# Half stores and tile order at the end, constants behind the input, two splits moved, and the norms' bias on VectorE

## The reference

```python
# first block, per layer l
y = _mla(x, ...) if l == 0 else _swa(x, ...)
x = _layernorm(alpha * x + y, ln_mix_g[l], ln_mix_b[l])
x = _layernorm(alpha * x + _mlp(x, mlp_w_up[l], mlp_w_down[l]), ln_mlp_g[l], ln_mlp_b[l])
# second block
h = rmsnorm(x, g[0]);  proj = h @ w_in
y = (gm * (hm @ w_mlstm_out) + gd * (hd @ w_diff_out) + gr * (hr @ w_ret_out)) @ w_out
x = x + rmsnorm(y, g[1])
h2 = rmsnorm(x, g[2]);  a, u = split(h2 @ w_ffn_in)
x = x + rmsnorm((silu(a) * u) @ w_ffn_out, g[3])
```

## Time and profile before

| | |
|---|---|
| Median of 3 runs | 2545.45 us (2542.76 to 2547.97) |
| Profiled execution | 2543.65 us |
| its span in the trace | 2541.9 us |
| TensorE matmuls | 2452.6 us, 96% |
| TensorE weight loads | 2024.5 us, 80% |
| VectorE | 1114.9 us, 44% |
| ScalarE | 886.0 us, 35% |
| Pool | 114.6 us, 5% |
| DMA | 220.32 MB, mean 87 GB/s |

### The profile page before, as it was taken

The page is one execution under the profiler, slowest core; times in us unless marked ns, Lnnn a source line. Parts: engine busy times, 40 slices in busy tenths (PEclk is TensorE's granted clock), DMA queues, the critical chain, the costliest instruction groups (busy, mean ns, idle before and its releaser), DMA issues.

```text
span 2541.9 us, 29499 instructions
## 1 busy us (share of the span) xinstructions
PE 2452.6 (96%) x11784; PEld 2024.5 (80%) x11784; DVE 1114.9 (44%) x1487; ACT 886.0 (35%) x1444; POOL 114.6 (5%) x169
## 2 busy tenths in 40 slices
PE   7798999999989999998999999999999999999997
PEld 7577888888878788887888888888877788888886
DVE  3355633445665543346455322223245524433334
ACT  3232422323443332235444323332245534522222
POOL 3000200000100100000000000000000000000001
PEclk9999999999999999999999999999999999999999
DMA  5512332222311323322222222222321122322221
GB/s 161 75 54 67 117 100 100 90 92 83 108 42 50 118 98 100 99 100 67 78 71 81 92 92 83 83 83 84 104 67 50 51 94 80 108 99 91 96 94 67
DMA packets 187063, 220.32 MB, mean 87 GB/s; under 512 B 20531, under 2 KB 141568, under 8 KB 186832
## 3 DMA queue, kind: packets, MB, share of 16 engines
q1 hardware_dynamic: 183200, 206.13, 25.4%
q0 software_dynamic: 3760, 12.73, 2.4%
HBM read 213.60 MB, written 5.24 MB: 86 GB/s over the span
## 4 chain that ended last, share of the span: by engine, by line
PE 89%; DVE 6%; ACT 3%; issue 1%; DMA 1%; POOL 0%; SPq 0%; ACTq 0%; POOLq 0%; DVEq 0%
PE A L507 46%; PE B L507 40%; DVE WL L1754 2%; PE C L507 1%; ACT WH L1186 1%; DMA X<-in_x 1%; DVE Y L1912 1%; PE C L876 0%; PE C L1091 0%; DVE YL L1969 0%; DVE st L1893 0%; PE C L932 0%; ACT ar L1262 0%; DVE ar L1967 0%; ACT XH L1189 0%
## 5 line engine op out<-in xcount | busy, mean ns | idle before, releaser
L1754 DVE TENSOR_TENSOR WL<-RAW,WH 128x2048 fp32r<-128x2048 f32 (+1 forms) x197 | 448.8, 2278 | 690.1 <-ACT WH L1186 690.1
L1186 ACT ACTIVATE WH<-RAW 128x2048 fp32r<-128x2048 f32 (+1 forms) x197 | 370.9, 1883 | 626.0 <-PE A L507 561.1
L507 PE MATMUL B<-XH,WH 128*128 128x512 f32 (+1 forms) x1440 | 548.2, 385 | 8.7 <-DVE WL L1754 5.4
L507 PE MATMUL B<-XH,WL 128*128 128x512 f32 (+1 forms) x1440 | 539.9, 379 | 0.0
L507 PE MATMUL B<-XL,WH 128*128 128x512 f32 (+1 forms) x1440 | 526.5, 381 | 6.4 <-DVE XL L1769 6.3
L507 PE MATMUL A<-WH,YH 128*128 128x512 f32 x944 | 367.7, 390 | 1.6 <-DVE YL L2243 1.6
L507 PE MATMUL A<-WH,YL 128*128 128x512 f32 x944 | 367.3, 389 | 0.0
L507 PE MATMUL A<-WL,YH 128*128 128x512 f32 x944 | 367.2, 389 | 0.0
L507 PEld LDWEIGHTS B<-XH,WH 128*128 128x128 f32 x1440 | 271.8, 189 | 78.2 <-issue 16.4
L507 PEld LDWEIGHTS B<-XH,WL 128*128 128x128 f32 x1440 | 272.0, 189 | 51.3
L507 PEld LDWEIGHTS B<-XL,WH 128*128 128x128 f32 x1440 | 263.7, 190 | 57.1 <-DVE XL L1769 8.3
(11 more groups left out here) (290 smaller groups left out, 2125.9 us busy)
## 6 DMA issues: line engine op xcount, KB each, us to landing
RAW<-in_w_in SPq DMA_DIRECT2D x33, 1024.0 KB, 5.1
RAW<-in_mlp_w_up SPq DMA_DIRECT2D x32, 1024.0 KB, 5.2
RAW<-in_mlp_w_down SPq DMA_DIRECT2D x32, 1024.0 KB, 5.0
RAW<-in_w_in SPq DMA_DIRECT2D x48, 512.0 KB, 4.3
RAW<-in_w_ffn_in SPq DMA_DIRECT2D x22, 1024.0 KB, 5.1
RAW<-in_w_ffn_out SPq DMA_DIRECT2D x10, 1024.0 KB, 5.0
RAW<-in_mla_w_o SPq DMA_DIRECT2D x4, 1024.0 KB, 5.1
RAW<-in_swa_w_q SPq DMA_DIRECT2D x4, 1024.0 KB, 4.9
```

The source lines that it names most:

```text
L507: return nc.tensor.matmul(dst, l, r, start=first, stop=last)
L1186: nc.scalar.activation(WH[s][:, 0:n], RAW[s][:, 0:n], ACT.Copy).then_inc(hi_ready, 1)
L1754: tt(WL[s][:, 0:n], RAW[s][:, 0:n], f32(WH[s][:, 0:n]), ALU.subtract).then_inc(lo_ready, 1)
```

## The change

- Pool waits for x's last tile before it issues the constants, and loads GB only behind the roots of the latents.
- `plus_bias` moves to VectorE: one tile behind each up weight tile's pair of features in the first group of both MLPs; at the SWA border two tiles behind each of two splits. Pool only waits and reloads GB.
- At the border to the in-projection ("pre"), the split of the first mLSTM weight tile moves on VectorE between the two halves of XL's low parts, on ScalarE ahead of tile 3's square.
- At the border to the FFN ("post"), the four low parts of the first half of XL move ahead of tile 3's product.
- In the last down half TensorE takes the token tiles in the order (t, kh) = (0,0), (1,0), (0,1), (1,1), (2,0), (2,1), (3,0), (3,1). The root is made by ScalarE and VectorE in place of Pool. VectorE multiplies the first half of Y by its gain in h = 0 (`first_half`), behind ScalarE's squares, and its split of the last weight tile moves behind the fourth add of h = 0. `add_normed` works in halves, and each half is stored by itself.

```diff
@@ -494,9 +494,11 @@
-            sp.wait_ge(s_("fin_x"), t + 1)
-            sp.dma_start(out[0, tok(t), :], X[:, t, :]).then_inc(s_("stored"), 16)
-        sp.wait_ge(s_("stored"), 16 * T)
+            for h in range(2):
+                cols = slice(512 * h, 512 * h + 512)
+                sp.wait_ge(s_("fin_x"), 2 * t + h + 1)
+                sp.dma_start(out[0, tok(t), cols], X[:, t, cols]).then_inc(s_("stored"), 16)
+        sp.wait_ge(s_("stored"), 16 * 2 * T)
...
@@ -1160,12 +1162,27 @@
             c, use, done = c + tiles, use + tiles, done + tiles
-            for h in range(2):
+            for h in range(2 if n < 2 else 1):
                 for kh in range(2):
...
                     c += 1
+        pe.wait_ge(lo_ready, c + 1)
+        for t, kh in ((0, 0), (1, 0), (0, 1), (1, 1), (2, 0), (2, 1), (3, 0), (3, 1)):
+            nk = (4, 2)[kh]
+            wh, wl = grid(WH[slot(c + kh)], nk, 512), grid(WL[slot(c + kh)], nk, 512)
+            if kh == 0:
+                pe.wait_ge(a_free[t], ra + 5)
+            elif t == 0:
+                pe.wait_ge(lo_ready, c + 2)
+            for j in range(nk):
+                k = 4 * kh + j
+                r = mm3(A[t][:], YH[:, k, tok(t)], YL[:, k, tok(t)], wh[:, j, :], wl[:, j, :], k == 0, k == 5)
+            if t == 3:
+                r.then_inc(chunk_done, 1)
+            elif kh:
+                r.then_inc(tok_done, 1)
...
@@ -1429,11 +1446,11 @@
         over_root("pre", 2)
+        split(BASE["if"][0] + 1)
         then_root("pre", 3)
...
-        split(BASE["if"][0] + 1)
         act.wait_ge(s_("if_abs"), 1)
...
@@ -1732,6 +1749,10 @@
                                      scale=D ** -0.5, accum_out=stat(SS + 4 * h + t)).then_inc(s_("fin_ss"), 1)
+                if h:
+                    act.wait_ge(s_("fin_ss"), T + t + 1)
+                    act.wait_ge(s_("fin_half"), t + 1)
+                    nc.scalar.activation(stat(RS + t), stat(SS + 4 + t), ACT.Sqrt, bias=stat(SS + t)).then_inc(s_("fin_root"), 1)
...
@@ -1933,6 +1954,7 @@
                 lo_half("pre", 0, (2, 3), NG0, ALU.mult)
+                split(c + 1)
                 lo_half("pre", 1, range(4), NG0, ALU.mult)
...
@@ -1955,6 +1977,10 @@
+        def plus_bias(t, dst, signal):
+            tt(dst[:, t, :], Y[:, t, :], GB[:, 1, :], ALU.add).then_inc(signal, 1)
         def mlp(name, before, ln, n):
...
@@ -1967,6 +1993,8 @@
                         tt(YL[:, 2 * j + m, :], SQ_T[:, m, :], f32(YH[:, 2 * j + m, :]), ALU.subtract).then_inc(mlp_lo, 1)
+                    if first:
+                        plus_bias(j, Y, s_(before + "_y"))
                 for h in range(2):
...
@@ -1999,12 +2027,16 @@
         split(c0 + 1)
+        for t in range(2):
+            plus_bias(t, X, s_("ln1_x"))
         for m in range(2):
...
         split(c0 + 2)
+        for t in range(2, T):
+            plus_bias(t, X, s_("ln1_x"))
         dve.wait_ge(chunk_done, c0 + 2)
...
@@ -2059,7 +2091,6 @@
         c0, _, _, _, _, f0 = BASE["if"]
-        split(c0 + 1)
         nc.vector.memset(L_PRE, 0.0).then_inc(s_("ml_zero"), 1)
...
@@ -2304,6 +2335,8 @@
         for t in range(T):
+            if t == 3:
+                lo_half("post", 0, range(4), NG2, ALU.mult)
             product_out(1, t)
...
@@ -2315,18 +2348,24 @@
             elif t == 3:
-                lo_half("post", 0, (0, 1), NG2, ALU.mult)
                 root_inverse("post", 3)
-                lo_half("post", 0, (2, 3), NG2, ALU.mult)
                 lo_half("post", 1, range(4), NG2, ALU.mult)
-        def add_normed(name, gb, t, after):
-            if t == 0:
-                dve.wait_ge(gb_in, gb)
-            dve.wait_ge(s_(name + "_r"), t + 1)
-            then(stt(Y[:, t, :], Y[:, t, :], stat(RS + t), GB[:, 0, :], ALU.mult, ALU.mult))
-            tt(X[:, t, :], X[:, t, :], Y[:, t, :], ALU.add).then_inc(s_(after), 1)
+        def first_half(t):
+            dve.wait_ge(s_("fin_ss"), t + 1)
+            then(tt(Y[:, t, 0:512], Y[:, t, 0:512], GB[:, 0, 0:512], ALU.mult))
+            ts(stat(SS + t), stat(SS + t), RMS_EPS, None, ALU.add).then_inc(s_("fin_half"), 1)
+        def add_normed(t):
+            dve.wait_ge(a_free[t], ra + 6)
+            then(tt(xtmp[:, t % 2, :], Y[:, t, 512:1024], GB[:, 0, 512:1024], ALU.mult))
+            dve.wait_ge(s_("fin_root"), t + 1)
+            then(nc.vector.reciprocal(stat(RS + t), stat(RS + t)))
+            for h, y in enumerate((Y[:, t, 0:512], xtmp[:, t % 2, :])):
+                x = X[:, t, 512 * h:512 * h + 512]
+                stt(x, y, stat(RS + t), x, ALU.mult, ALU.add).then_inc(s_("fin_x"), 1)
...
@@ -2346,8 +2385,9 @@
             for h in range(2):
-                split(c + 1)
-                split(c + 2)
+                if n < 2 or h == 0:
+                    split(c + 1)
+                    split(c + 2)
                 for t in range(T):
...
@@ -2355,10 +2395,19 @@
                         tt(y, y, A[t][:], ALU.add).then_inc(a_free[t], 1)
-                    if n == 2 and h == 1 and t >= 1:
-                        add_normed("fin", 4 * 32 + 32, t - 1, "fin_x")
+                    if n == 2 and h == 0 and t == 0:
+                        dve.wait_ge(gb_in, 4 * 32 + 32)
+                    elif n == 2 and h == 0:
+                        if t == 3:
+                            split(c + 3)
+                        else:
+                            first_half(t - 1)
+                    elif n == 2:
+                        if t == 0:
+                            first_half(2)
+                            first_half(3)
+                        add_normed(t)
                 c += 2
-        add_normed("fin", 4 * 32 + 32, T - 1, "fin_x")
...
@@ -2378,6 +2427,8 @@
             return v.rearrange("(a n) -> a n", a=1)
+        pool.wait_ge(x_in[T - 1], 16)
...
@@ -2408,8 +2459,6 @@
-        load_gb(a["ln_mix_g"][0], a["ln_mix_b"][0])
         def over_root(dst, src, eps, signal):
...
@@ -2420,17 +2469,10 @@
+        load_gb(a["ln_mix_g"][0], a["ln_mix_b"][0])
         pool.wait_ge(consts_done, 1)
...
-        def plus_bias(ln, dst, signal):
-            pool.wait_ge(turned, turn(ln, KD))
-            for t in range(T):
-                tt(dst[:, t, :], Y[:, t, :], GB[:, 1, :], ALU.add).then_inc(signal, 1)
-        pool.wait_ge(chunk_done, BASE["mlp0"][0] + 1)
-        plus_bias("ln0", Y, s_("ln0_y"))
         pool.wait_ge(s_("ln0_y"), T)
...
@@ -2443,14 +2485,11 @@
         load_bias(1)
-        plus_bias("ln1", X, s_("ln1_x"))
         pool.wait_ge(s_("ln1_x"), T)
...
             load_bias(g)
-        pool.wait_ge(chunk_done, BASE["mlp1"][0] + 1)
-        plus_bias("ln2", Y, s_("ln2_y"))
         pool.wait_ge(s_("ln2_y"), T)
...
@@ -2479,16 +2518,8 @@
-        def root_of_halves(name, wait, t):
-            wait(t)
-            then(tt(stat(SS + t), stat(SS + t), stat(SS + 4 + t), ALU.add))
-            over_root(RS + t, SS + t, RMS_EPS, s_(name + "_r"))
         pool.wait_ge(s_("post_x"), T)
         load_gb(a["norm_gains_2"][0, 3])
-        for t in range(T):
-            root_of_halves("fin", lambda t: pool.wait_ge(s_("fin_ss"), T + t + 1), t)
...
```

## The result

| | median | range | runs |
|---|---|---|---|
| before | 2544.11 us | 2542.66 to 2547.97 | 4 |
| after | 2525.07 us | 2523.35 to 2526.57 | 4 |

The ratio is 0.9923, with a 95% interval of 0.9905 to 0.9940: 19 us less. The prediction was 2525.5 us.

What follows compares the result with a forecast made beforehand. TensorE, busy 2452.6 of 2541.9 us, was taken as the bound of nearly every stage. Terms 5.0 + 4.0 + 2.4 + 3.9 + 0.1 + 3.4 = 18.8 us gave 2524.9 from the profiled execution; forecast 2525.5, range 2518 to 2533.

Steps and rivals of the forecast that it cites:

- Start: Wait for x at the kernel's start: constants issued behind x let its tiles land earlier; 5.0 us, range 2 to 6.
- the rule: At the start: Pool's DMAs can starve beside two-port VectorE operations; constants would come late but within their cover, costing nothing.
- Bias: Both MLPs: bias adds on VectorE end TensorE's wait for a split stretched by Pool; 4.0 us in MLP 0, 2.4 in MLP 1.
- SWA border: Bias adds moved to VectorE at this border, where no TensorE wait stands: nothing gained, bounds -1 to +1 us.
- Border to the in-projection: Earlier split of the first mLSTM weight tile ends TensorE's wait for the gate op; 3.9 us, 2.2 if the clock falls anyway.
- FFN border: Low parts ahead of product 3: TensorE's wait is cut in two and moved; 0.1 us, bounds -0.5 to +0.5.
- The end: Tail behind the last matmul: VectorE's chain sets the end, with a new 2.6 us TensorE idle; 3.4 us gained.
- SP's slow queue (1): Rival at the start: SP's own queue is the slow one; 3 us less gain, 2528.5 us, chance 0.15.
- the missing wait (2): Rival at the end: the new wait is absent, tile 0 ends 2.6 us earlier; 2523 us, chance 0.12.
- the pushed split (3): Rival in both MLPs: VectorE's adds still push a split past TensorE's need; 6.4 us less, 2532 us, chance 0.08.
- the clock (4): Rival in the pair stage: TensorE's clock stays at the lower level for some 25 us; above 2550 us, chance 0.03.

Runs made afterwards that it cites:

- pool_dummy: The kernel after, with Pool also making four adds of the same size in MLP 0 that nobody needs; 2529.10 us.
- fix_post: The kernel after, with the low parts at the FFN border made in two pieces around the last product; 2527.75 us.
- u_pre: The kernel after, with the split at the in-projection border put back where before has it, on VectorE and ScalarE; 2528.11 us.
- fix_if: The kernel after, with ScalarE's split behind the gates' Exp and Ln and VectorE's behind the last gate operation; 2525.25 us.
- fix_end2: The kernel after, with VectorE's last weight split behind its second add and each tile finished behind the next tile's add; 2521.78 us.
- u_start: The kernel after, with the start of before: Pool issues the constants at once, ahead of x's tile 3; 2531.36 us.
- only_end: The kernel before, with nothing but the new end; 2538.03 us over ten runs.
- gb_only: The kernel before, with only the two GB loads moved behind Pool's roots; 2542.13 us.
- u_bias: The kernel after, with the three sets of four bias adds given back to Pool; 2534.66 us.

## Why the prediction held

The predicted 18.8 us stand against 19.6 us in the profiled pair and 19.0 in the medians. (The 2525.5 lies between 2524.9, from the profiled execution, and 2526.7, from the median; with a fourth run the median of before is 2544.11, 0.5 above the profiled one in place of 1.8.) Step by step:

**Start.** Predicted 5.0, with up to 1 us more; shown about 6, and 6.5 in the profiled pair (6.15 at the mark, where after has 1.7 us more of falls). The steps came 0.3 us late each: tile 3's transposes at 11.92 against 11.6, the first matmul at 13.84 against 13.5. What I had left in the range, that the first matmuls run at full rate at once, came true and is worth more than the 1 us: of the 6.5 us, 4.7 are the earlier first matmul and 1.9 the rate behind it. This term was mis-sized. The reasoning by bytes was right in direction and too neat: bytes at 285 GB/s give 3.0 of the 4.6 us, and GB, over half of the bytes, did nothing. In after the constants are issued from 11.6 to 22.2 us, at 0.49 to 0.70 us each beside VectorE's splits, no longer than in before (0.49 to 0.76). The prediction drew the rule too wide: the Trainium skill ("SBUF — State Buffer", Who interferes with whom) ties the starving to operations in a two-port mode and says that `tensor_tensor`, which these splits are, has none. The trace of after agrees. Nothing waited for a constant.

**Bias.** MLP 0 predicted 4.0, shown 4.4 with the SWA border, of which MLP 0 up to its last down product is 4.1; MLP 1 predicted 2.4, shown 2.5. The idle and the stretched split went as walked. The doubt in that step, whether the clock falls elsewhere instead, is answered below. The rows show what the stretch is: a stretched operation ends about its own length behind the Pool add beside it. In the earlier trace rows the last Pool add ends at 290.03 and the split, begun at 287.70, ends 2.15 us later (its own length is 2.29); in pool_dummy it is 283.42 and 1.08 us later (1.22). So what is added is the rest of a Pool add, here 2.2 us at most (2.88, 3.42 and 4.48 against 0.69, 1.22 and 2.29). The Trainium skill ("SBUF — State Buffer", SBUF: two separate sides) calls the sharing an exclusive lock held for the whole instruction, and the trace agrees.

**SWA border.** Predicted 0 (-1 to 1), and 0.3 shown. The -1.57 behind it is falls: that stretch takes 18.8 to 22.3 us in the fourteen profiled kernels, in no relation to their edits.

**Border to the in-projection.** Predicted 3.9, shown 1.8. This is the step that failed. I reckoned the gate operation a microsecond ahead of TensorE's need and stopped there; I did not ask what is late next. It is ScalarE's exponential, at the end of a chain from the gate operation over two weight splits and two scans. The chain moved by 1.8 us, and TensorE, 3.9 us earlier, waits 2.1 us for it. In the old order it waits 1.6 us there without a fall and not at all with one, so the fall's 1.7 us, a term of the 3.9, had cost nothing, and of the 2.2 us of idle 0.5 came back. That the profiled pair still showed 4.04 up to that point is chance: before had 5.1 us of falls there, 3.4 of them ahead of the idle, and after none.

**FFN border.** Predicted 0.1, shown 0.3, with the wait in two pieces as said (0.84 and 1.05).

**The end.** Predicted 3.4, between 4.0 without a fall behind the new idle and 2.8 with one; shown 3.7, without one. Sizes: the idle 2.33 us against 2.6, a tile 3.39 us against 3.25 (VectorE waits 0.46 us in each for ScalarE's root), the span's end 2.5 us behind the last write against 3.0. Counted from the last part's first matmul, the last write came 0.9 us later than reckoned, and the shorter time behind it gave 0.5 of that back. A fall behind the idle came in four other kernels: in fix_post, where it begins with the idle's end, it costs 1.2 us, as reckoned; in u_pre, pool_dummy and fix_if, where it begins 1.3 us later, 0.1 to 0.2 us. That VectorE's chain sets the end was right, and fix_end2 showed it to be VectorE's work even without its waits.

For the profiled pair the parts are 6.5 + 4.4 + 2.5 + 1.8 + 0.3 + 3.7 = 19.2 us, and the 0.4 us to its 19.6 are what falls come to elsewhere. That the sum came out is in part luck: the border's 2.1 us too much stand against 1.5 too little at the start, 0.4 in MLP 0, 0.1 in MLP 1, 0.2 at the FFN border and 0.3 at the end. Of the rivals, SP's slow queue (1) fell with u_start, the missing wait (2) with the 2.33 us, the pushed split (3) with the rows of MLP 0, and of the clock (4) nothing came beyond what moves any two runs apart.

## What to carry to other kernels

When an edit removes a wait, follow the work it releases to the same engine's next wait: a chain on two other engines can stand just behind, and a slow clock in the profiled run can hide it. Value an edit of a few microseconds by the stretch between two marks that both kernels have, at equal falls of the clock; here the whole time moves by 4 us for no reason of the edit. Compare the same matmul in both traces where no mark stands. Put an operation that waits for another engine behind the work that a third engine needs next, and keep Pool's long adds away from a VectorE whose work is due.

## What had not been expected of the hardware

**A fall that belongs to an idle.** The idle of 2.2 to 3.4 us in MLP 0 is followed by a fall of the granted clock in all five profiled kernels that have it (before, only_end, gb_only, u_bias, pool_dummy), and there is none there in the nine others. In windows of MLP 0 (busy time of PE, PEld, DVE, ACT and POOL with the instructions, then the granted clock, the DMA share and GB/s) u_bias has

```profile
286.00:291.00 5.00, 4.43 (x13) 3.50 (x14) 3.10 (x5) 2.97 (x4) 2.62 (x4) 0.68 0.96 298
```

and after

```profile
286.00:291.00 5.00, 5.00 (x24) 4.14 (x23) 4.69 (x4) 2.60 (x3) 0.00 (x0) 1.00 0.00 0
```

so the idle costs 2.2 us and the fall behind it 1.7. The idle of 2.21 us in MLP 1 has no fall in any of four kernels, and that of 2.33 us at the end has one in four of nine. What sets these apart isn't settled.

**Falls make the spread.** With TensorE's clock at the lower of its two levels, 1.2 in place of 2.4 GHz, the granted clock of the profiled executions lacks 15.3 to 23.9 us behind the start. Fix_post and after are the same up to the mark near 205 us and reach it at 209.48 and 205.26, though their 61st matmuls start at 18.90 and 18.95; their falls from there to the mark are 11.9 and 6.8 us. What a fall lacks isn't always lost: the 1.7 us behind the gate idle of before cost nothing, and three of the four at the end 0.1 to 0.2 us.

**Pool's adds are dear for others.** Four adds of 128x1024, 10.8 us on Pool and of no use to anybody, cost 5.3 us between the marks of MLP 0: 3.35 of idle TensorE, 1.7 of the fall behind it, and the rest small.
